# Mixture of experts in a two-layer diffusion step: one expert's weights outside the ring, one row list per layer, straight-line expert loops

## The reference

```python
def expert_block(args):
    xi, e = args
    hid = jax.nn.silu(xi @ w1[e]) * (xi @ w3[e])     # (rows, 1024) @ (1024, 512), twice
    return hid @ w2[e]                                # (rows, 512) @ (512, 1024)
# x = x + g2 * hier_moe(rms_norm(x, g_ffn) * (1 + sc2) + sh2, ...)
```

## Time and profile before

| what | value |
|---|---|
| median of 3 runs | 1748.03 us (1746.92 to 1750.51) |
| profiled execution, its own time | 1745.22 us |
| span of its records | 1743.4 us |
| PE busy / PEld busy | 1552.1 us (89%) / 740.9 us (42%) |
| DVE / ACT / POOL busy | 452.7 / 296.7 / 145.3 us |
| granted PE clock, mean | 0.934 |
| moved by DMA | 522.14 MB, mean 299 GB/s |

### The profile page before, as it was taken

How to read it: one execution, slowest core, us unless ns; L and a number is a source line. 1 busy time by engine, 2 the same in 40 slices (tenths; PEclk the granted TensorE clock), 3 DMA queues, 4 the chain that set the end, 5 groups by cost and what they waited for, 6 DMA issues and landing times.

```text
span 1743.4 us, 21453 instructions
## 1 busy us (share of the span) xinstructions
PE 1552.1 (89%) x8414; PEld 740.9 (42%) x8414; DVE 452.7 (26%) x1063; ACT 296.7 (17%) x597; POOL 145.3 (8%) x199
## 2 busy tenths in 40 slices
PE   4899877797999999999967998796999999999991
PEld 3445765444344444334423444444434443334440
DVE  0212275623311111111113023633311111111113
ACT  1100112511111111111112003521111111111112
POOL 1101103000000000000014000010000000000000
PEclk9899977797999999999987998997899999999996
DMA  9977954014999999999979422023599999999992
GB/s 348 259 262 268 330 203 163 7 70 179 419 423 423 423 423 423 424 424 424 423 285 300 168 99 85 1 77 133 203 421 424 424 423 423 424 425 422 424 387 112
DMA packets 99382, 522.14 MB, mean 299 GB/s; under 512 B 10090, under 2 KB 11562, under 8 KB 56320
## 3 DMA queue, kind: packets, MB, share of 16 engines
q1 hardware_dynamic: 85920, 485.58, 68.9%
q0 software_dynamic: 13408, 35.81, 6.5%
HBM read 511.60 MB, written 20.22 MB: 305 GB/s over the span
## 4 chain that ended last, share of the span: by engine, by line
PE 83%; DVE 9%; DMA 3%; ACT 2%; issue 1%; SPq 1%; POOL 0%; DVEq 0%; POOLq 0%; ACTq 0%
PE psum L831 25%; PE psum L519 14%; PE psum L844 13%; PE psum L812 10%; PE psum L777 5%; PE psum L837 3%; PE psum L824 2%; PE psum L818 2%; PE psum L462 2%; DMA ring<-in_ada_w 1%; PE psum L787 1%; PE psum L705 1%; PE psum L692 1%; DVE area_q L1219 1%; DVE small L1229 1%
## 5 line engine op out<-in xcount | busy, mean ns | idle before, releaser
L831 PE MATMUL psum<-ring,area_t 128*64 128x512 f32 x1024 | 451.8, 594 | 2.9 <-issue 1.2
L832 PE MATMUL psum<-ring,area_t 128*64 128x512 f32 x1024 | 452.1, 595 | 0.0
L831 PEld LDWEIGHTS psum<-ring,area_t 128*64 128x64 f32 x1024 | 139.8, 137 | 293.9 <-issue 292.7
L519 PE MATMUL psum<-ring,area_t 128*128 128x512 f32 (+1 forms) x576 | 242.5, 583 | 0.0
L844 PE MATMUL psum<-ring,area_t 128*64 128x512 f32 x1024 | 233.9, 599 | 2.2 <-DVE area_t L1704 2.2
L1675 DVE COPY area_q<-psum 64x512 f32<-64x512 f32 x64 | 44.5, 695 | 573.4 <-PE psum L832 573.3
L812 PE MATMUL psum<-area_h,area_t 128*64 128x512 f32 x768 | 181.1, 607 | 3.0 <-DVE area_t L1689 3.0
L519 PEld LDWEIGHTS psum<-ring,area_t 128*128 128x128 f32 x576 | 110.3, 193 | 128.1 <-issue 126.3
L1881 POOL DMA_INDIRECT pair_rows<-area_q,idx x64 | 62.3, 973 | 941.2 <-ACT area_q L1137 926.6
L832 PEld LDWEIGHTS psum<-ring,area_t 128*64 128x64 f32 x1024 | 140.0, 138 | 0.0
L844 PEld LDWEIGHTS psum<-ring,area_t 128*64 128x64 f32 x1024 | 68.2, 136 | 119.3 <-issue 111.8
(11 more groups left out here) (242 smaller groups left out, 1303.6 us busy)
## 6 DMA issues: line engine op xcount, KB each, us to landing
ring<-in_moe_w SPq DMA_DIRECT2D x192, 2048.0 KB, 16.0
ring<-in_ada_w SPq DMA_DIRECT2D x24, 2048.0 KB, 16.5
ring<-in_na_w_in SPq DMA_DIRECT2D x6, 2048.0 KB, 18.5
ring<-in_ab_w_in SPq DMA_DIRECT2D x5, 2048.0 KB, 11.0
area_m<-mod_ready POOLq DMA_DIRECT2D x6, 1024.0 KB, 9.5
area_q<-pair_rows POOLq DMA_DIRECT2D x6, 1024.0 KB, 7.0
ring<-in_ab_w_out SPq DMA_DIRECT2D x2, 2048.0 KB, 15.3
area_g<-mod_ready POOLq DMA_DIRECT2D x4, 1024.0 KB, 7.9
```

What stands on the lines that cost most here:

```text
L519: mm = pe.matmul(banks[2 + g % 4][:, 0:w], hT[:, k, t * P:t * P + P], wchunk(n, KT)[:, k, 0:w], start=(k == 0), stop=(k == KT - 1))
L831: pe.matmul(banks[2 + u][0:64, :], lhsT, w1[:, k, :], start=(k == 0), stop=(k == KT - 1))
L832: mm = pe.matmul(banks[2 + u][64:128, :], lhsT, w3[:, k, :], start=(k == 0), stop=(k == KT - 1))
```

## The change

- **SPARE = 2.** The chunks of expert 2 of each layer leave the ring. They go to memory that is free at that time: w1 to rows of the projections that nobody reads after the output product (`area_q`), w3 and w2 to the memory of the modulation vectors (`area_m`, `area_g`). SP issues them after the chunks of experts 0 and 1: w1 after `out_done`, w2 (two halves) after `x_mixed`, w3 after `h_ready`. Expert 3 takes the ring's place of expert 2, so the ring's later chunks are one expert further on.
- POOL's loads of the modulation vectors go to that same memory, so they move from before the experts to behind the scatter of expert 2, after a wait for its down products.
- **Rows once per layer.** `rank_slots` on DVE makes two selection matrices `slots` for the first and second choice of each token, `places` on PE multiplies them once with the pair numbers of all 32 experts (6 products, in expert 0), `index` on DVE makes all row lists. The 3 products and the integer conversion per expert go.
- `pick` compares 64 slots per token group and not 128.
- **Loops written out** on PE, ACT, DVE and SP. `weigh` runs after expert 12.

```diff
+SPARE = 2
+        slots = area_q[:, 3352:4120].rearrange("p (k t s) -> p k t s", k=2, t=NT)
+        spare = [area_q[:, 5120:9216], area_m[:, 0:4096], (area_m[:, 4096:6144], area_g[:, :])]
-            stream += [("moe", l, c) for c in range(3 * EXPERTS)]
+            stream += [("moe", l, c) for c in range(3 * EXPERTS) if c // 3 != SPARE]
...
+            def load_spare(l):
+                def piece(dst, src):
+                    sp.dma_start(dst, src).then_inc(spare_landed, 16)
+                sp.wait_ge(S["out_done"], (l + 1) * NT * OUT_CHUNKS)
+                piece(expert_dst(spare[0], 0), expert_dram(l, SPARE, 0))
+                sp.wait_ge(S["x_mixed"], (l + 1) * NT * OUT_CHUNKS)
+                w2 = expert_dram(l, SPARE, 2)
+                for half in range(2):
+                    piece(spare[2][half], w2[:, 2048 * half:2048 * half + 2048])
+                sp.wait_ge(S["h_ready"], NT * (2 * l + 2))
+                piece(expert_dst(spare[1], 1), expert_dram(l, SPARE, 1))
             def load_experts(l):
-                with sp.Fori(1, EXPERTS // 2) as i:
-                    for u in range(2):
-                        one(sp.snap(i * 2 + u), u)
+                for e in range(EXPERTS):
+                    if e == SPARE:
+                        load_spare(l)
+                        continue
+                    for j in range(3):
+                        n = NUM["moe", l, 3 * e + j]
+                        load(n, expert_dst(ring[:, place(n), :], j), expert_dram(l, e, j))
...
-                index_products([(sel[u][:, t, :], column[t]) for t in range(NT)]).then_inc(M["index_done"], 1)
+            def places(l):
+                pe.wait_ge(S["slots_ready"], l + 1)
+                for k in range(2):
+                    for t in range(NT):
+                        mm = pe.matmul(banks[5][:, 0:EXPERTS], slots[:, k, t, :], val[k][:, t, :],
+                                       start=(k == 0 and t == 0), stop=(k == 1 and t == NT - 1))
+                mm.then_inc(S["places_done"], 1)
...
+            def rank_slots(l):
+                for k, (oh, rank) in enumerate(((o1, m1), (o2, m2))):
+                    ts(pval[:, k, :], keep[:, KEEP["pair"]], 2.0 * k, None, ALU.add)
+                    tt(val[k], oh, last(pval[:, k, :], EXPERTS), ALU.mult)
+                    tt(c32, oh, key, ALU.mult)
+                    red(rank, c32, ALU.add)
+                    tt(slots[:, k, :, :], lead(keep[:, KEEP["slot"]], NT), last(rank, P), ALU.is_equal,
+                       "dve_step" if k == 0 else "slots_ready")
...
-                pool.wait_ge(S["x_mixed"], NT * OUT_CHUNKS * (l + 1))
-                load_G(l, 1)
-                pool.wait_ge(S["h_ready"], NT * (2 * l + 2))
-                if l == 0:
-                    load_AB(1, 0)
-                else:
-                    get(modA[:, 0, :], spread(a["norm_final"]), "gfin_loaded")
                 base = l * EXPERTS
+                pool.wait_ge(S["places_ready"], l + 1)
                 for e in range(EXPERTS):
-                    scatter(M, e, e % 2, base, l)
+                    scatter(M, e, e % 2, base, l, idx[:, e:e + 1])
+                    if e == SPARE:
+                        pool.wait_ge(M["y_done"], base + SPARE + 1)
+                        load_G(l, 1)
+                        if l == 0:
+                            load_AB(1, 0)
+                        else:
+                            get(modA[:, 0, :], spread(a["norm_final"]), "gfin_loaded")
```

More of the change, by code:

```diff
@@ L331, in expert_dram @@
         def expert_dram(l, e, j):
-            one = (l, e) if isinstance(e, int) else (l, bass.ds(e, 1))
             if j == 2:
@@ L838, in hidden_turns, with down_products @@
                 return mm
[L840 removed]
+            def down_products(u, rows):
                 for k in range(4):
@@ new lines, in experts @@
+            def experts(l):
+                tokens(l, 0)
+                turn_tokens(l, 0)
+                for e in range(EXPERTS):
+                    if e == SPARE:
+                        up = [spare[j].rearrange("p (k n) -> p k n", k=KT) for j in range(2)]
+                        halves = [v.rearrange("p (k n) -> p k n", k=2) for v in spare[2]]
+                        rows = [halves[k // 2][:, k % 2, :] for k in range(4)]
+                        pe.wait_ge(spare_landed, 64 * (l + 1))
+                    else:
+                        ns = [NUM["moe", l, 3 * e + j] for j in range(3)]
+                        up = [wchunk(ns[j], KT) for j in range(2)]
+                        rows = [wchunk(ns[2], 4)[:, k, :] for k in range(4)]
+                        for j in range(2):
+                            pe.wait_ge(landed[place(ns[j])], when(ns[j]))
+                    hidden(l, e, *up)
+                    if e + 1 < EXPERTS:
+                        tokens(l, e + 1)
+                    turn_hidden(l, e)
+                    if e + 1 < EXPERTS:
+                        turn_tokens(l, e + 1)
+                    if e == 0:
+                        places(l)
+                    if e != SPARE:
+                        pe.wait_ge(landed[place(ns[2])], when(ns[2]))
+                    down(l, e, rows)
@@ L1150, in experts @@
             def experts(l):
-                base = l * EXPERTS
-                copy_tokens(0, base)
-                one(0, 0, base)
-                one(1, 1, base)
-                with act.Fori(1, EXPERTS // 2 - 1) as i:
-                    for u in range(2):
-                        one(act.snap(i * 2 + u), u, base)
-                one(EXPERTS - 2, 0, base)
-                one(EXPERTS - 1, 1, base, last=True)
+                copy_tokens(l, 0)
+                for e in range(EXPERTS):
+                    one(l, e)
                 act.wait_ge(S["over_ready"], l + 1)
@@ L1618, in route @@
                 tt(d3, m2, m1, ALU.subtract, "route_exp")
-                stt(val, o2, 2.0, last(keep[:, KEEP["pair"]], EXPERTS), ALU.mult, ALU.add)
-                for k in range(2):
-                    ts(pval[:, k, :], keep[:, KEEP["pair"]], 2.0 * k, None, ALU.add)
                 v.wait_ge(S["ranks_done"], l + 1)
@@ L1683, in pick @@
-            def pick(e, u, base):
-                if not (isinstance(e, int) and e < 2):
-                    v.wait_ge(M["index_done"], e + (base - 1))
-                rank = key[:, :, e] if isinstance(e, int) else key[:, :, bass.ds(e, 1)].rearrange("p t e -> p (t e)")
-                v.tensor_tensor(sel[u], lead(keep[:, KEEP["slot"]], NT), last(rank, P), ALU.is_equal)\
-                    .then_inc(M["sel_ready"], 1)
-            def index(e, u, base):
-                v.wait_ge(M["index_done"], e + (base + 1))
-                if not (isinstance(e, int) and e + base < 2):
-                    v.wait_ge(M[f"scattered{u}"], scat(e, u, base) - 16)
-                v.tensor_scalar(idx[u][:, :], banks[5][:, 0:1], keep[:, KEEP["skip"]], None, ALU.add)\
-                    .then_inc(M["index_ready"], 1)
@@ L1700, in product, with one @@
[L1700 to L1703 removed]
+            def one(l, e):
+                u, E = e % 2, l * EXPERTS + e
+                v.wait_ge(M["hid_done"], E + 1)
+                if E >= 2:
+                    v.wait_ge(M["hidT_done"], E - 1)
+                v.tensor_copy(hs[u][64:128, :], banks[2 + u][64:128, :]).then_inc(M["up_copied"], 1)
@@ new lines, in tokens, with pick @@
+            def tokens(l, e):
+                u, E = e % 2, l * EXPERTS + e
+                v.wait_ge(M["xT_done"], E + 1)
+                if E >= 2:
+                    v.wait_ge(M["hid_done"], E - 1)
+                v.tensor_copy(xT[u][:, :, :].rearrange("p k s -> p (k s)"), banks[1][:, :]).then_inc(M["xT_copied"], 1)
+            def pick(l, e):
+                u, E = e % 2, l * EXPERTS + e
+                if e >= 2:
+                    v.wait_ge(M["tok_done"], E - 1)
+                v.tensor_tensor(sel[u][:, :, 0:BLOCK], lead(keep[:, KEEP["slot"]][:, 0:BLOCK], NT),
+                                last(key[:, :, e], BLOCK), ALU.is_equal).then_inc(M["sel_ready"], 1)
```

229 lines of the change are left out of this document (91 added, 138 removed).

## The result

The change costs time. In the first comparison the changed kernel took 1757.91 us (median of 4 runs, 1756.72 to 1760.53) and the kernel before 1747.47 us (1745.42 to 1750.51), a ratio of 1.0061 with an interval of 1.0037 to 1.0084. Forecast were +3.1 us, and 1744 to 1768 us as the range. Two executions far above all others, 7846 us in e1 and 1938 us in e3 (the latter at a granted clock of 0.813), are left out as slow ones.

The account below looks back on a forecast made before the run. The experts were taken as bound by PE, the ring just behind. Stalls of 4.4 us in layer 0 and 1.35 in layer 1, against 2.25 before, gave +3.5, with picks +3.1: 1751.1 us; range 1744 to 1768.

Parts of the forecast that it names:

- waits for the ring: PE waiting for weights late in layer 0, from expert 20 or so on: 4 to 5 us.
- index products: Three PE products an expert removed: in the shadow of transposes, ACT and DVE, so 0 (bounds 0 and -0.26 us an expert).
- places products: Six products on PE in expert 0, in place of the three there, covered by the same rows: 0.
- packets: PE's 16 KB instruction fetches within the experts delay one DMA engine: one hit a layer, +1.0 us (bounds 0 and 13).
- the fast rival: Index products were in PE's path and the ring can keep 14.99 us an expert: -10.8 us, 1737; chance 0.08.
- Expert 2 outside the ring: Expert 2's weights load in little-used DMA time before the experts; the ring's lag shrinks: -1.0 us a layer.
- POOL's loads: Modulation loads behind expert 2 get in the ring's way: +3.5 us in layer 0 (bounds 0 and +7.4), 0 in layer 1.
- The one-engine rival: All PE instruction packets use one DMA engine, 8.6 us a layer within the experts: +18.3 us, 1766; chance 0.30.
- Picks: The first pick before each layer's experts, with half the elements: -0.2 us a layer (bounds for both together 0 and -0.5).
- Pace 14.84: Sign of being right: PE's gathers still 14.84 us apart early in a layer.
- L844 0.2 us behind DVE's product: Sign of being right: w2's weight load on PE still starts 0.2 us after DVE's product ends.
- idle DMA stretch: Sign of being right: DMA engines idle near 467 to 474 us, in layer 0's experts.

Follow-up runs that it names:

- e1: The changed kernel again, unaltered; ratio 1.0037 (1.0018 to 1.0056) to the kernel before.
- e3: The changed kernel with expert 2 back in the ring and POOL's loads back in front of the experts; ratio 1.0041 to the kernel before.
- e8: The changed kernel with PE's experts 4 to 29 looped, places products early, expert 2 in the ring, POOL's loads in front; ratio 0.9997 to the kernel before.
- e6: The kernel before with the loops of SP, ACT and DVE written out and PE's kept; ratio 0.9995 to the kernel before.
- e11: The changed kernel with slot ranks found earlier and places products between the first gather and its transposes; ratio 1.0039 to the kernel before.
- e12: The kernel of e7 measured again, unaltered; ratio 1.0016 to the kernel before.
- e7: The changed kernel with PE's experts 4 to 29 looped, POOL's loads at the layer's end and places products early; ratio 1.0010 to the kernel before.
- e10: The changed kernel with POOL's loads moved from behind expert 2 to behind the last expert's hidden products; ratio 1.0032 to the kernel before.
- e4: The changed kernel with only PE's experts 4 to 29 in a loop of two again; ratio 1.0000 to the kernel before.
- e2: The kernel before with only its four expert loops (PE, SP, ACT, DVE) written out; ratio 1.0037 to the kernel before.
- e5: The kernel before with only PE's expert loop written out; ratio 1.0018 to the kernel before.

## Why the prediction was right, and where it was not

The direction, the mechanism and the range held, and the size was low: +3.1 forecast, +6.5 (3.2 to 9.8) measured. Within the experts the sum can be laid beside its own terms. Against the prediction's 30 x 14.835 = 445.05 us, layer 0 had 4.4 us of loss forecast and 449.74 - 445.05 = 4.7 measured; layer 1 had 1.35 forecast and 2.6 measured. Together 7.3 against 5.75. That is close, but several terms were wrong and cancelled, and this part is luck: against the faster pace the waits for the ring were 6.6 us in layer 0, where 4 to 5 were forecast, and 4.5 in layer 1. The steps of the prediction that failed in size are the index products, the places products and the packets; the first two were put at nothing.

- **Index products: "I take 0".** They were worth 0.09 us an expert on PE, some 2.7 us a layer, since the transposes behind them and not DVE's product held w2's load. The bounds (0 to -0.26) held. The total is still nothing, for the reason given in the fast rival: the ring takes it back. e8 has no index products and PE at 14.74, e6 has them at 14.84, and S0 + S1 are 893.93 and 893.57 us, with e8's places products not even in its sum. No run took the index products away alone.
- **Places products: "the same rows cover: 0".** Wrong. Those rows stand for 3 products ahead of the transposes; 6 behind them lie open. 15.71 - 14.74 = 0.97 us a layer. e11 takes 0.9 and 0.8 of it out of the sums, but only to in front of them: there it costs 0.6 to 0.9 us.
- **Expert 2 outside the ring, -1.0 a layer.** Right in sign. It measured -1.75 in layer 1 (e3 against e1) and, with loops on PE, +0.5 to +0.9 in layer 0 and +3.4 to +3.7 in layer 1 for taking it away (e8 against e12 and e7, where the place of POOL's loads differs too).
- **POOL's loads, +3.5 in layer 0, 0 in layer 1.** The delay of w2 that e10 takes away is 3.0 us at that chunk and 1.8 one expert later; at the end of the layer it is worth 1.1 us. With expert 2's gain the prediction had +2.5 net in layer 0, and e3 against e1 gives +0.8.
- **Instruction packets, one hit a layer at +1.0 us.** The mechanism was right: one 16 KB packet holds one engine for 1.06 us, and the ring is behind from there on only now and then. The size was low. A hit moves the landing by 1.1 to 2.0 us, there are one to two in a layer, and in the two profiles of the changed kernel they fall on the same experts. In the sums PE's written-out code costs 2.6 us in the changed kernel (e1 against e4), 2.8 (e2 against e6) and 7.8 (e5 against before).
- **The one-engine rival** (+18.3) is refuted: hits come one packet in about eight where the spacing could be read (e5), not every time. In the part of e5 before the stalls, the landing grew 0.3 us an expert but for the hit.
- **Picks, -0.2 a layer.** Right. Two picks now take 0.63 us instead of the 1.03 of the earlier trace rows, but the first gather waits for the first alone: in the chain it takes 0.37 us instead of 0.57, in both layers.
- **Pace 14.84, L844 0.2 us behind DVE's product** were named as signs; they read 14.74 and 0.07. The idle DMA stretch, w3 at 16.4 us, packets every 27 us (30 forecast) and waits from expert 19 on read about as forecast.

**What stays open.** S0 + S1 are 5.1 us (e1: 4.8) above before, the picks give 0.4 back, and the median says 6.5, within an interval of 3.3 us to either side. Five kernels with all four engines written out have a mean ratio of 1.0037, the five measurements with PE alone in a loop 1.0004: 0.33%, 5.9 us, where the sums of e1 against e4 and of e2 against e6 differ by 2.6 and 2.8 us. So either written-out PE code also costs something outside the experts, or the scatter there hides what the sums show. The "rest" of the profiles, 851 to 863 us for one and the same kernel, is too wide to decide it with one profile each: its mean is 855.6 us over the seven profiles with PE in a loop and 857.1 us over the seven with PE written out. No run was made for that. So it is shown that PE's written-out code costs the time; that the ring's landings carry it is shown for about half.

The Trainium skill, "Runtime: NRT & Kernel Launch", section "Instruction fetch mechanics", calls the crossing of a 16 KiB boundary "mostly hidden" and names branches as what stalls. The runs differ with it: PE in a loop has a ratio of 1.0000 (e4), written out 1.0037 (e1), and the loop's steps are 14.74 us, the same as the written-out ones. Within the experts the fetch is hidden from PE itself. It is not hidden from the transfers that share the DMA engines.

## What to carry to other kernels

Where a kernel keeps the DMA engines at 100%, the instruction stream is one more load on them: leave the engine with the most instructions in a loop, and price written-out code by the landing of the transfers beside it, not by the engine that runs it. Where PE and a ring of loads are level, a gain on PE alone is given back within the stage; both sides have to be eased. Before two profiles are compared by their spans, find a stretch that repeats to tenths of a microsecond in two profiles of the same kernel, and compare that. Then look at what an edit moved across the ends of that stretch: three microseconds that e7 gained inside it had gone to just before and just behind it.

## What the runs showed of the hardware that was not expected

- Two profiles of one kernel: spans of 1743.4 and 1755.6 us, the 892 us of dense work equal to 0.2 us. The first gather lay between 417.9 and 426.6 us over 14 profiles, and the last down products took either 3.67 us (17 of 28 layers) or 5.36 to 5.37 us (11 of 28, six of them with PE written out and five with its loop).
- The granted clock can stay low into dense work. In e8, whose first gather took 5.20 us, the window around the first hidden products is at 0.57, and they took up to 1.06 us each where they otherwise take 0.59. From the first hidden product to the second gather it was 8.59 us instead of 6.89. It is not e8's own: six of 28 layers have 8.6 us there, layer 1 of the kernel before among them, and the other 22 have 6.89. The window:

```profile
432.00:436.00 4.00, 3.56 (x10) 1.39 (x12) 0.45 (x2) 0.00 (x0) 0.00 (x0) 0.57 0.00 0
```

- An instruction packet of 16 KB takes 1.06 us of one DMA engine, and with PE written out the 2 MB transfers whose landing stepped beside one came 1.1 to 2.0 us later; most packets do not show in any landing. In e2, e3 and e5 the ones that did were eight packets apart, in both layers.
